# Inverse levels of a blocked recurrence: correcting one matrix form by products and turning the other from it

## The reference

```
def step(S, inp):
    r_t, w_t, k_t, v_t, kk_t, a_t = inp
    s_kk = jnp.einsum('zbhvk,zbhk->zbhv', S, kk_t)
    S = (S * w_t[..., None, :] - s_kk[..., None] * (kk_t * a_t)[..., None, :]
         + v_t[..., :, None] * k_t[..., None, :])
    return S, jnp.einsum('zbhvk,zbhk->zbhv', S, r_t)
```

## Time and profile before

| | |
|---|---|
| median of 3 runs | 2598.05 us (2597.29 to 2607.45) |
| profiled execution, its own time | 2604.03 us |
| its span | 2602.2 us |
| mean granted clock of TensorE | 0.965 |
| PE busy | 2373.7 us (91%), 19518 records |
| DVE busy | 1800.2 us (69%) |
| ACT busy | 1254.0 us (48%) |
| copies with mask, L1430 | 180 of 732 ns, 131.2 us |
| records of L899, L903, L916 (products of the inverse) | 2400 each, 106.5, 103.0 and 100.3 us |

### The profile page before, as it was taken

One profiled execution on the slowest core, in us unless ns is written; L12 is line 12 of the kernel. 1 busy time (PEld: TensorE's weight loads), 2 busy tenths in 40 slices (PEclk: granted clock), 3 DMA queues, 4 the chain that ended last, 5 costly groups with the idle time before them and its releaser, 6 DMA issues. The chain is left out here.

```text
span 2602.2 us, 51685 instructions
## 1 busy us (share of the span) xinstructions
PE 2373.7 (91%) x19518; PEld 1584.5 (61%) x19518; DVE 1800.2 (69%) x2293; ACT 1254.0 (48%) x1545; POOL 151.4 (6%) x160
## 2 busy tenths in 40 slices
PE   5987999999999789699999999899896999999996
PEld 2435776767676665466666666555554666666665
DVE  2344665756575621799999999469416999999994
ACT  2021323232323210488888788301304878888882
POOL 1000000000000000000000000000000000000000
PEclk8998999999999999899999999899897999999998
DMA  9852010101010011799999999401007999999993
GB/s 372 324 219 104 3 31 3 31 3 31 3 31 3 20 51 41 269 385 388 385 384 390 389 386 364 148 36 65 0 1 264 373 385 384 392 387 388 384 384 91
DMA packets 176368, 539.35 MB, mean 207 GB/s; under 512 B 12417, under 2 KB 48897, under 8 KB 176066
## 3 DMA queue, kind: packets, MB, share of 16 engines
q1 hardware_dynamic: 169666, 514.63, 51.6%
q0 software_dynamic: 6528, 22.29, 3.7%
HBM read 510.29 MB, written 26.61 MB: 206 GB/s over the span
## 5 line engine op out<-in xcount | busy, mean ns | idle before, releaser
L1928 DVE TENSOR_TENSOR wl<-raw,wh 128x1024 fp32r<-128x1024 f32 x768 | 897.7, 1222 | 76.0 <-DVEq L1927 68.0
L1870 ACT ACTIVATE wh<-raw 128x1024 fp32r<-128x1024 f32 x768 | 796.2, 1058 | 233.7 <-ACTq L1869 228.1
L1803 PE MATMUL ps<-wh,xs 128*80 128x512 f32 x3072 | 844.9, 393 | 4.6 <-PEq L1798 4.6
L1803 PEld LDWEIGHTS ps<-wh,xs 128*80 128x80 f32 x3072 | 449.6, 148 | 243.5 <-issue 5.4
L1803 PE MATMUL ps<-wl,xs 128*80 128x512 f32 x1536 | 476.5, 391 | 0.0
L1803 PEld LDWEIGHTS ps<-wl,xs 128*80 128x80 f32 x1536 | 227.3, 148 | 127.1 <-issue 0.4
L1430 DVE COPY_PREDICATED wk<-m,ps 128x512 f32<-128x512 uint8 x180 | 131.2, 732 | 110.6 <-DVEq L1429 109.6
L773 PE MATMUL ps<-h,wk 128*128 128x512 f32 (+1 forms) x576 | 184.3, 463 | 3.1 <-PEq L1037 3.1
L1153 ACT ACTIVATE wk<-ps 128x256 f32<-128x256 f32 (+1 forms) x180 | 65.8, 366 | 201.0 <-ACTq L1152 201.0
L773 PEld LDWEIGHTS ps<-h,wk 128*128 128x128 f32 x576 | 97.5, 199 | 82.5 <-issue 79.5
L2047 PE MATMUL ps<-h,wk 128*128 128x512 f32 (+1 forms) x448 | 123.7, 438 | 3.3 <-PEq L2038 3.3
(11 more groups left out here) (285 smaller groups left out, 2745.3 us busy)
## 6 DMA issues: line engine op xcount, KB each, us to landing
raw<-in_moe_w_gate SPq DMA_DIRECT2D x64, 2048.0 KB, 10.5
raw<-in_moe_w_up SPq DMA_DIRECT2D x64, 2048.0 KB
raw<-in_moe_w_down SPq DMA_DIRECT2D x64, 2048.0 KB, 12.8
wk<-in_mod_w SPq DMA_DIRECT2D x24, 2048.0 KB, 11.1
wk<-in_ev_w_in SPq DMA_DIRECT2D x18, 512.0 KB, 4.9
wk<-in_od_w_in SPq DMA_DIRECT2D x4, 2048.0 KB, 14.8
ysum<-raw SPq DMA_DIRECT2D x10, 512.0 KB, 17.1
hrow<-rows SPq DMA_DIRECT2D x10, 512.0 KB, 7.0
```

The costliest lines, as they stand in the source:

```text
L1803: last = pe.matmul(ps[0:CAP, b0 + k], lhs[:, xk, c, :], w[:, s, a:b], start=c == 0 and xk == 0 and w is wh, stop=c == KC - 1 and xk == 1)
L1870: act.activation(wh[:, n % SPLIT], raw[:, n // 4 % RAW, n % 4], ACT.Copy).then_inc(sem("high_ready"), 1)
L1928: dve.tensor_tensor(wl[:, n % SPLIT], raw[:, n // 4 % RAW, n % 4], wh[:, n % SPLIT].bitcast(F32), ALU.subtract).then_inc(sem("low_ready"), 1)
```

## The change

Only the transposed inverse is now kept through the levels, in `xt`, with half the size of `xx`, and corrected by products. The plain one, `xn`, is made from it in every slot: `turn(q)` transposes two 128x128 tiles on PE (both blocks of a head lie beside each other, both heads below each other), and ACT copies them (`copy_xn`). `correct` has 8 matmuls instead of 16. The head hh, and no longer the block k, selects the half of the partitions, in `xt`, `yw` and the results. `middle` writes bank 2 or 3 by its block and stands three slots behind `correct` instead of two, so a pass has 33 slots on PE instead of 32. At level 0 `correct_first` has 4 wider matmuls with 128 rows. The masked copy has 256 columns. The corner copies go together in two groups, of two and of three tiles, and the block copies are 4 instead of 10.

```diff
@@ -648,7 +648,8 @@
             mix, lora, wk = work["mix"], work["lora"], work["area"]
             ca = Carve()
             mat = ca(NT, 2, 2, 4, P)
-            xx = ca(NT, 2, 2, 2, HD)
+            xt = ca(NT, 2, 2, HD)
+            xn = ca(NT, 2, 2, HD)
             yw = ca(NT, 2, 2, HD)
...
-            invT = lambda g, z, hh, lo, hi: xx[lo:hi, g, z, 0, hh]
-            inv = lambda g, z, hh, lo, hi: xx[lo:hi, g, 1 - z, 1, hh]
-            slotT = lambda z, hh: z * 2 * HD + hh * HD
-            slotN = lambda z, hh: (1 - z) * 2 * HD + hh * HD
+            HALF = ((0, HD), (HD, P))
+            on = lambda half: slice(*HALF[half])
+            slot = lambda z, k: slice((z * 2 + k) * HD, (z * 2 + k + 1) * HD)
             zbank = lambda q: (4, 6)[q % 2]
-            corner_bank = (0, 1, 6, 7, 0)
+            nbank = lambda q: (5, 7)[q % 2]
+            CORNERS = ((0, 2, 0), (2, NT, 6))
...
+                        def correct_first(q):
+
+                            upto("x_new", q - 1)
+                            for k in range(2):
+                                for hh in range(2):
+                                    last = pe.matmul(ps[on(hh), zbank(q), 0:4 * HD].rearrange("p (z k n) -> p z k n", z=2, k=2)[:, :, k], ident[:, on(k)],
+                                                     mat[:, q, :, hh, 0, on(k)], start=True, stop=True)
+                            last.then_inc(sem("z_ready"), 1)
+
                         def correct(q):
 
-                            g, zb = q % NT, zbank(q)
+                            g = q % NT
                             upto("x_new", q - 1)
-                            if q >= NT:
-                                upto("yw_copied", q - NT + 1)
+                            upto("yw_copied", q - NT + 1)
                             for z in range(2):
-                                for hh in range(2):
-                                    for k, (lo, hi) in enumerate(HALF):
-                                        to, te = (lo, hi) if q >= NT else HALF[1 - k]
-                                        lhs, rhs = (yw[lo:hi, g, z, hh], invT(g, z, hh, lo, hi)) if q >= NT else (eye64[lo:hi], mat[lo:hi, g, z, hh, 0, lo:hi])
-                                        pe.matmul(ps[to:te, zb, slotT(z, hh):slotT(z, hh) + HD], lhs, rhs, start=True, stop=True)
-                                    for k, (lo, hi) in enumerate(HALF):
-                                        to, te = HALF[1 - k] if q >= NT else (lo, hi)
-                                        lhs, rhs = (invT(g, z, hh, lo, hi), yw[lo:hi, g, z, hh]) if q >= NT else (mat[lo:hi, g, z, hh, 0, lo:hi], eye64[lo:hi])
-                                        last = pe.matmul(ps[to:te, zb + 1, slotN(z, hh):slotN(z, hh) + HD], lhs, rhs, start=True, stop=True)
+                                for k in range(2):
+                                    for hh in range(2):
+                                        last = pe.matmul(ps[on(hh), zbank(q), slot(z, k)], yw[on(hh), g, k, z], xt[on(hh), g, z, k], start=True, stop=True)
                             last.then_inc(sem("z_ready"), 1)
 
                         def middle(u):
 
                             g = u % NT
-                            upto("x_new", u + 1)
-                            upto("yw_copied", u - 1)
+                            upto("xn_copied", u + 1)
+                            upto("yw_copied", u)
                             for z in range(2):
-                                for hh in range(2):
-                                    for k, (lo, hi) in enumerate(HALF):
-                                        to, te = HALF[1 - k]
-                                        at = (z * 2 + hh) * HD
-                                        last = pe.matmul(ps[to:te, 2 + u % 2, at:at + HD], mat[lo:hi, g, z, hh, 0, lo:hi], inv(g, z, hh, lo, hi), start=True, stop=True)
+                                for c in range(2):
+                                    for hh in range(2):
+                                        k = hh ^ c
+                                        last = pe.matmul(ps[on(hh), 2 + k, z * HD:(z + 1) * HD], mat[on(k), g, z, hh, 0, on(k)], xn[on(k), g, z, hh], start=True, stop=True)
                             last.then_inc(sem("yw_ready"), 1)
 
                         def corner_middle(u):
 
                             g = u % NT
-                            upto("x_new", u + 1)
-                            upto("yw_copied", u - 1)
+                            upto("xn_copied", u + 1)
+                            upto("yw_copied", u)
                             for hh in range(2):
-                                for z, (lo, hi) in enumerate(HALF):
-                                    to, te = HALF[1 - z]
-                                    last = pe.matmul(ps[lo:hi, 2 + u % 2, hh * HD:(hh + 1) * HD], mat[lo:hi, g, z, hh, 0, to:te], inv(g, z, hh, lo, hi), start=True, stop=True)
+                                for z in range(2):
+                                    last = pe.matmul(ps[on(hh), 2 + z, 0:HD], mat[on(z), g, z, hh, 0, on(1 - z)], xn[on(z), g, z, hh], start=True, stop=True)
                             last.then_inc(sem("yw_ready"), 1)
 
+                        def turn(q):
+
+                            upto("x_new", q + 1)
+                            for z in range(2):
+                                last = pe.transpose(ps[:, nbank(q), z * P:(z + 1) * P], xt[:, q % NT, z].rearrange("p k n -> p (k n)"), ident)
+                            last.then_inc(sem("xn_ready"), 1)
+
                         def corner(g):
 
                             upto("yw_copied", NZ - NT + g + 1)
-                            if g == NT - 1:
-                                pe.wait_ge(sem("corner_copied"), 1).then_inc(sem("corner_copied"), -1)
+                            first, end, bank = CORNERS[g >= CORNERS[1][0]]
                             for hh in range(2):
-                                for z, (lo, hi) in enumerate(HALF):
-                                    last = pe.matmul(ps[lo:hi, corner_bank[g], hh * HD:(hh + 1) * HD], yw[lo:hi, g, 0, hh], invT(g, z, hh, lo, hi), start=True, stop=True)
-                            last.then_inc(sem("corner_ready"), 1)
-
-                        for q in range(NZ + 2):
-                            if q < NZ:
+                                for z in range(2):
+                                    at = (g - first) * HD
+                                    last = pe.matmul(ps[on(z), bank + hh, at:at + HD], yw[on(hh), g, z, 0], xt[on(hh), g, z, 1 - z], start=True, stop=True)
+                            if g == end - 1:
+                                last.then_inc(sem("corner_ready"), 1)
+
+                        for q in range(NZ + 3):
+                            if q < NT:
+                                correct_first(q)
+                            elif q < NZ:
                                 correct(q)
-                            if 0 <= q - 2 < NZ - NT:
-                                middle(q - 2)
-                            elif q >= 2:
-                                corner_middle(q - 2)
-                            if q == NZ:
+                            if 3 <= q < NZ - NT + 3:
+                                middle(q - 3)
+                            elif q >= NZ - NT + 3:
+                                corner_middle(q - 3)
+                            if 1 <= q <= NZ:
+                                turn(q - 1)
+                            if q == NZ + 1:
                                 if following:
                                     slot_read()
                                 corner(0)
+                                corner(1)
                             if q == 2:
                                 pe.wait_ge(sem("r_copied"), 1).then_inc(sem("r_copied"), -1)
                             if following and q == 2:
                                 take_weights()
                             if following and q % 3 == 2 and q < 3 * KC:
                                 project(K, 0, (q // 3,))
-                        corner(1)
                         corner(2)
+                        corner(3)
+                        keep_busy(pe, 4, 3)
+                        corner(4)
                         if following:
                             for a, b in halves:
                                 last = pe.matmul(pair(2)[:, a:b], w2[0:HD, 0], lora[0:HD, 0, a:b], start=True, stop=True)
                             last.then_inc(sem("e_ready"), 1)
                         else:
-                            keep_busy(pe, 5, 3)
-                        corner(3)
-                        corner(4)
-                        keep_busy(pe, 2, 4)
-                        pe.wait_ge(sem("corner_copied"), 4).then_inc(sem("corner_copied"), -4)
+                            keep_busy(pe, 4, 4)
+                        pe.wait_ge(sem("corner_copied"), 2).then_inc(sem("corner_copied"), -2)
```

(40 more changed lines are left out.)

5 lines of the change are left out of this document (2 added, 3 removed).

## The result

The changed kernel takes 2613.58 us (median of 17 runs, 2606.99 to 2631.11), the kernel before on the same chip 2605.62 us (17 runs, 2596.33 to 2616.64): ratio 1.0045, 95% interval 1.0029 to 1.006. I had forecast 2586 and 2568 to 2612. The profiled execution took 2611.37 us with a span of 2609.6 us, 7.4 more than before (2604.0 and 2602.2).

A forecast was written before the change was run, and what follows sets the result against it. TensorE was taken to pace the inverse's slots, its instructions arriving no faster than some 64 per us. Five passes +5, last pass -7, ends -3 and clock -7 sum to -12: 2598 becomes 2586 us, range 2568 to 2612.

The forecast's parts named there:

- Both are below 64, so the standing still goes: Inverse's new slots: TensorE instructions at 56 per us (last pass) and 45 (others) stay under the supply limit, so stalls end.
- some 64 per us: TensorE stalls "until issue" in the last pass, some 256 instructions (4 us) apart, read as a limit on instruction supply.
- The prediction's own sign of being wrong: The forecast is wrong if TensorE's stalls appear at 50 instructions per us too.
- Slot 1.21 us, triple 4.71: Inverse on TensorE: a slot grows from 0.93 to 1.21 us, three slots with a projection chunk from 4.24 to 4.71.
- F: Rival: two row tiles cannot use one PSUM bank at a time in the new `correct`; +73, 2671 us, chance 0.01.
- Last pass -7: Inverse's last pass, without projection: first to last masked copy falls from 43.1 to 36.0 us.
- Five passes +5: Inverse's five passes with projection: masked copies take 44.4 us each against 43.4, +1.0 a pass.
- Ends -3: Inverse's end, last masked copy to first state product: 5.3 us against 6.0, 0.5 taken as saved in each of six passes.
- Clock -7: Stage of the states in the five projecting passes: most falls to 1.2 GHz go, returning 7 of 12 us.
- D: Slower rival: stalls are not instruction supply, or supply slows at shape changes; 3.3 us (five passes) and 7 (last) remain; 2616, chance 0.09.
- E: Slower rival: the inverse runs at 1.2 GHz, its slots about 2.1 us; +160, 2750 us, chance 0.05.
- the prediction's last sign of being wrong: The forecast is wrong if TensorE's clock falls inside the inverse.

The follow-up runs named there:

- The probe: All of the kernel's stages left out, TensorE alone running the same 4096 instructions of 64x64 matmuls without waits: 54.86 us written out, 35.14 as a loop.

## Why the prediction was wrong

The step that failed is "**Both are below 64, so the standing still goes**", and with it "I read that as TensorE's instructions not arriving faster than some 64 per us". The places were right, 256 instructions apart. But from the distance in one stretch I took a rate; it was the work of 256 instructions plus a wait. With waits counted in, a slot before has 98 instructions in 0.93 us: 256 take 2.43 us, + 1.5 = 4.0. After it has 71 in 1.21: 256 take 4.36, + 1.5 = 5.9, as measured. A rate of 64 would have given 4.0 and 4.36. The change took fewer, longer slots and kept the price per 256. The prediction's own sign of being wrong, stalls at 50 instructions per us too, came at 43 to 45.

- **Slot 1.21 us, triple 4.71**: right, 1.21 and 4.72. Changes of shape cost 0.09 us each, three times as often too. Two row tiles in one bank run side by side (14 records of `correct` in 0.62 us), so F falls: the row held against the Trainium skill's Gotcha 1.
- **Last pass -7**: got -0.9. 29 x 1.21 + 0.44 = 35.5; the five gaps, less the 0.058 that a start would take anyway, are 6.9, together 42.4 against 42.2.
- **Five passes +5**: got +19.3. The work was right: of the missing 14 us the stops make 11.1 and the clock's falls inside the inverse an estimated 3.2, and what is left is 222 us, the forecast. (8 x 4.71 + 5 x 1.21 + 0.3 + 0.47 is 44.5, not 44.4; nothing hangs on it.)
- **Ends -3**: got -1.1. I took the saving from the second pass, which does go from 6.0 to 5.4, and multiplied by six; it had the longest end before, and the others save between -0.1 and 0.4. The end on its own, without the turn, gives -6.9.
- **Clock -7**: -11.5 in the profiled pair, about -6 by the mean clocks of the runs. The mechanism is borne out in part: the fillers alone bring all of it back in one profiled execution, and 5 us in the median.
- **Sign and size**: 0.09 for D, 2616, was too little. D's gaps (3.3 and 7 us) are close to what stayed (2.2 a pass, and 7.0); measured 2613.58. My argument against D, "the stalls' distance counted in instructions", fits a price per 256 as well as a rate and told nothing between them. The whole loss is then this: forecast with a rate 0 of gaps, measured 18 us of them, and the states' clock gave back part.
- E did not happen as a whole: the clock in the masked copies' windows is 0.97 to 1.00. But it did fall inside the inverse, the prediction's last sign of being wrong, for 3.4 us behind the 1.93 us stop of the fourth pass.

The Trainium skill, "Runtime: NRT & Kernel Launch", section "Instruction fetch mechanics", says that the sequencer fetches 16 KiB blocks of 256 instructions by its own DMA queue while it executes the current one, and that crossing to the next is mostly hidden. The blocks agree with the trace (16384 bytes, every 256th); the hiding does not, for short matmuls: 1.5 us of 4.0 stood open. The Trainium skill also says there that a taken branch to a block outside the current two stops the engine for a fetch, and that kernels therefore prefer to be written out. The probe's loop of 128 instructions never leaves what was fetched once, and was 20 us faster than the same work written out.

## What to carry to other kernels

When an engine stops "until issue" at a fixed count of instructions, find the packet that comes in and take its wait as a price per count, to be added to the work of that count unless long work is queued just ahead; before calling it a rate, look at two stretches with different work per instruction. Trading many short matmuls for fewer and longer slots saves only that price per instruction removed (here 0.57 - 0.42 us a slot, by 1.5 us per 256), and pays the slot's growth in full (0.28). A change of several parts should be timed part by part: its small one, the corner copies in groups, was worth 17 us and was hidden under the large one's 25.

## What the runs showed of the hardware

- A block of 256 TensorE instructions costs a stop of 1.3 to 2.1 us in a stream of 64x64 matmuls written out, 2.3 to 2.6 us from the packet's start to the first matmul out of it; a loop of 128 instructions fetches once and never stops.
- A projection chunk of 1.08 us in the stretch ahead of the block's end removes most of the stop (six of 35 places over 0.3 us, 3.5 us in sum and not 11.1); less so where the block ends inside the chunk (0.54 and 0.96 us, where 0.80 and 1.62 had been).
- 1.22 us of standing still ahead of L980 came before a granted clock of 0.92 over the next 43.5 us in the second pass (part of it at the 1.2 GHz level), and of 1.00 in the first; with five more fillers there it was 1.00, the 2.4 GHz level, in all five passes of the one profiled execution.
